# The copies of the bias tables from memory to memory: four parts of two heads instead of one copy of eight

## What is computed

```python
h = rms_norm(x, norm_gain)
proj = h @ w_in              # pool value, pool gate, q, k, v, attention gate: 512 columns each
y_pool = multiscale_pool(pool_v, pool_w, pool_scale) * silu(pool_g)
# each chunk of 64 rows reads itself and 8 chunks before it, 8 heads of 64
s = q @ k.T / 8 + bias[h, clip(j - i, -64, 64) + 64]
y_attn = softmax(masked s) @ v * silu(attn_g)
out = rms_norm(x + concat(y_pool, y_attn) @ w_out, final_norm_gain)
```

## Time and profile before

| | |
|---|---|
| median of 3 runs | 1805.46 us (1803.0 to 1809.53) |
| profiled execution, its own time | 1807.35 us |
| span of the profile | 1805.6 us |
| granted TensorE clock, mean | 0.984 of full speed |
| busy share: TensorE, VectorE, ScalarE, GpSimd | 91%, 59%, 47%, 39% |
| traffic of the DMA engines | 257.84 MB, mean 143 GB/s |

### The profile page before, as it was taken

How to read it: one execution, slowest core, us unless ns; L and a number is a source line. 1 busy time by engine, 2 the same in 40 slices (tenths; PEclk the granted TensorE clock), 3 DMA queues, 4 the chain that set the end, 5 groups by cost and what they waited for, 6 DMA issues and landing times. The chain is left out here.

```text
span 1805.6 us, 43913 instructions
## 1 busy us (share of the span) xinstructions
PE 1644.2 (91%) x17920; PEld 1220.5 (68%) x17920; DVE 1068.5 (59%) x2188; ACT 843.5 (47%) x1580; POOL 708.4 (39%) x734
## 2 busy tenths in 40 slices
PE   5999699999999999999879999999999999999977
PEld 2554345568667676777567787778777787778854
DVE  7767477747456556544355565556655565556654
ACT  5554455422112111111145766567565765667565
POOL 3534345311112121001324644465545654456544
PEclk8999899999999999999989999999999999999999
DMA  5655574462542453244743342442334332442332
GB/s 205 209 204 200 196 247 170 170 251 72 186 164 83 163 187 129 83 159 166 218 147 101 99 131 79 136 131 106 102 106 148 112 125 72 136 148 90 107 94 83
DMA packets 111231, 257.84 MB, mean 143 GB/s; under 512 B 11928, under 2 KB 24744, under 8 KB 108984
## 3 DMA queue, kind: packets, MB, share of 16 engines
q1 hardware_dynamic: 109992, 253.73, 42.0%
q0 software_dynamic: 1040, 1.31, 0.4%
HBM read 151.33 MB, written 83.48 MB: 130 GB/s over the span
## 5 line engine op out<-in xcount | busy, mean ns | idle before, releaser
L2029 POOL TENSOR_TENSOR stages<-stages 128x512 f16<-128x512 f32 (+1 forms) x368 | 379.3, 1046 | 445.3 <-ACT stages L1814 445.1
L1489 PE MATMUL bank<-middle,weights 128*128 128x128 f16 x1792 | 315.0, 220 | 14.0 <-DVE middle L1526 13.1
L1492 PE MATMUL bank<-middle,weights 128*128 128x128 f16 x1792 | 314.6, 220 | 0.0
L1491 PE MATMUL bank<-middle,weights 128*128 128x128 f16 x1792 | 314.5, 220 | 0.0
L1808 ACT ACTIVATE stages<-bank,log_ps 128x512 f32<-128x512 f32 (+1 forms) x368 | 222.0, 603 | 163.9 <-POOL stages L2029 93.4
L1899 DVE CUSTOM_DVE_ANT_0 stages<-bank,stages 128x640 bf16<-128x640 f32 (+4 forms) x256 | 200.0, 781 | 158.2 <-PE bank L1647 157.9
L975 PE MATMUL bank<-middle 128*128 128x256 f16 x784 | 215.7, 275 | 7.5 <-DVE stages L1103 7.5
L977 PE MATMUL bank<-middle 128*128 128x256 f16 x784 | 215.7, 275 | 0.0
L978 PE MATMUL bank<-middle 128*128 128x256 f16 x784 | 215.6, 275 | 0.0
L1677 PE MATMUL bank<-middle 128*128 128x128 f16 (+1 forms) x840 | 169.4, 244 | 46.5 <-ACT stages L1808 41.9
L1814 ACT ACTIVATE stages<-stages 128x512 f16<-128x512 f32 (+1 forms) x368 | 203.5, 553 | 11.7
(11 more groups left out here) (147 smaller groups left out, 3544.3 us busy)
## 6 DMA issues: line engine op xcount, KB each, us to landing
entry<-in_x SPq DMA_DIRECT2D x64, 512.0 KB, 3.6
h_ops<-middle SPq DMA_DIRECT2D x16, 1792.0 KB, 6.1
middle<-h_ops SPq DMA_DIRECT2D x112, 256.0 KB, 5.1
middle<-h_ops SPq DMA_DIRECT2D x49, 512.0 KB, 6.9
middle<-middle SPq DMA_DIRECT2D x192, 128.0 KB, 2.3
residual<-entry SPq DMA_DIRECT2D x32, 512.0 KB, 2.8
entry<-residual SPq DMA_DIRECT2D x30, 512.0 KB, 4.1
out<-entry SPq DMA_DIRECT2D x30, 512.0 KB, 2.9
```

Source lines behind the costliest of these rows:

```text
L1489: nc.tensor.matmul(dst, wh, hop3[:, o, 0, kt, :], start=(kt == 0 and s < 2 and pair == 0), stop=False, skip_group_check=True)
L1491: nc.tensor.matmul(dst, wh, hop3[:, o, 1, kt, :], start=False, stop=False, skip_group_check=True)
L1492: mm = nc.tensor.matmul(dst, wl, hop3[:, o, 0, kt, :], start=False, stop=(kt == 3), skip_group_check=True)
L2029: nc.gpsimd.tensor_tensor(p_l[:, h % 2, c + a:c + b], p32[:, s, a:b], p_h[:, h % 2, c + a:c + b], ALU.subtract).then_inc(A["pl_done"], 1)
```

## The change

The two copies of all eight heads at the end of turn 5 become four pairs of copies of two heads each, at the ends of turns 5, 6, 7 and 8, each at the same place, behind `store_v(p, 1)` and ahead of the next turn's `load_x`. Each DMA is built as before, but its outermost dimension has 2 entries (heads) in place of 8. The semaphore `bias_stored` now reaches 128 instead of 32, and both waits for it ask for that.

```diff
+            def store_bias(h):
+
+                if h == 0:
+                    sp.wait_ge(H["ext_stored"], 16)
+                for r, (dst, width) in enumerate(((bq_dram, 640), (bk_dram, 256))):
+                    sp.dma_start(dst[h:h + 2], bass.AP(rel_dram.tensor, (r * HEADS + h) * EXT + P - 1,
+                                               [[EXT, 2], [-1, P], [1, width]])).then_inc(H["bias_stored"], 16)
...
-                if p == BIAS_AT + 2:
-                    sp.wait_ge(H["ext_stored"], 16)
-                    for r, (dst, width) in enumerate(((bq_dram, 640), (bk_dram, 256))):
-                        sp.dma_start(dst, bass.AP(rel_dram.tensor, r * HEADS * EXT + P - 1,
-                                                  [[EXT, HEADS], [-1, P], [1, width]])).then_inc(H["bias_stored"], 16)
+                if 0 <= p - BIAS_AT - 2 < HEADS // 2:
+                    store_bias(2 * (p - BIAS_AT - 2))
...
-            pool.wait_ge(H["bias_stored"], 32)
+            pool.wait_ge(H["bias_stored"], 16 * HEADS)
...
-            sp.wait_ge(H["bias_stored"], 32)
+            sp.wait_ge(H["bias_stored"], 16 * HEADS)
```

## The result

The changed kernel takes 1856.74 us (median of 4 runs, 1855.41 to 1858.74) against 1806.38 for the one before: ratio 1.028, 95% interval 1.0258 to 1.0302. The forecast was 1855.4. The profiled execution has a span of 1857.0 us, 51.4 more than before, at a mean granted clock of 0.968 instead of 0.984.

What follows compares the result with a forecast made beforehand. TensorE bounds the first stage unless held; the copies' late x load holds it. Three added delays put turn 10 at 48.4 us later, plus 1.5 slow clock: 1807.35 + 49.9 = 1857.3, 1855.4 as a median; range 1836 to 1868.

Steps and rivals of the forecast that it cites:

- One head to an engine: Bias copies: each head's share runs on one engine at 25 GB/s, so a two-head part still takes 19.1 us.
- the first rival: Copy division at line 867: parts keep eight engines or more, each delaying 4.8 us, 1796.5 us as a median; chance 0.08.
- The loop of A, B and C: Turns 6 to 9: three lengths chain each late square to the next store; turn 10 begins 49.9 us later.
- A: From the store of h to the next turn's square: 28.35 us with the copies, 9.60 or 8.89 without.
- B: From that square to the start of TensorE's next turn when it has to wait: 6.47 us.
- C: From TensorE's start of a turn to the next store of h: 2.22 us, some 3.4 in turn 9.
- The fold turn's hole at the transposes: Turn 7, line 240: TensorE's second transposes wait for the copy-out behind the square, starting at 229.5 instead of 214.76.
- The other rivals: Bias parts: two engines run faster than 25 GB/s each, 1817 us, chance 0.04; delays cancel, 1803 to 1809, chance 0.02.
- The lower bound: Least time of a bias part: 0.92 MB over all 16 engines at 393 GB/s, 2.3 us, inside the slack of 3.
- the forecast case: Four parts at turns 5 to 8, each delaying the x load 19.1 us: 1855.4 us as a median; chance 0.86.
- the faster rival: Same as the first rival: eight engines gain 8.9 us by turn 10, all 16 gain 17.5 (1788); chance 0.08.
- What queues behind the part: SyncE's queue: x load, gates store, second x load, in turns 6 and 9 two weight loads; only first x load late.

Runs made afterwards that it cites:

- the single narrow part: Against the kernel before: heads 0 and 1 alone copied at the end of turn 5, other six heads in four 12-wide parts, turns 6 to 9; 1811.32 us, ratio 1.0015.

## Why the prediction was right, step by step

- *One head to an engine, so a part costs its 19 us whatever its bytes.* This step carried the case. Shown by the shares 0.13, 0.26 and 0.51 to 0.52 for two, four and eight heads, by the single narrow part (hole 15.46) and by the same bytes in the shape of eight (holes under 3). The rule on the number of engines in the Trainium skill (page "DMA: Bandwidth & Descriptors", section "Why a DMA increments its semaphore by 16 and not by 1") pointed the same way, and all three shares agree with it; the first rival (eight engines whatever the shape) fell.
- *The loop of A, B and C.* Square of turn 7: forecast 227.3, measured 226.75. Transposes: 229.5 and 229.01. Square of turn 8: 266.4 and 265.45. Turn 9: 272.9 and 271.93. Square of turn 9: 304.3 and 303.06. Turn 10: 310.8 and 309.52. The length A was 0.5, 1.0 and 0.3 us shorter than put, and the stretch from turn 7's transposes to the store of h 0.5 longer (8.77 against 8.27). The sum was 49.9; the mark of turn 10 moved by 49.3, of which 0.5 was there before turn 6 (its first transposes begin at 166.55, before at 166.03). That the two numbers lie so close is in part luck: the start of turn 10 was put 1.3 us too late, and its slow matmuls, put at 1.5 us, cost 2.2 (from 309.52 to the mark are 4.78 us, in the kernel before 2.59).
- *The fold turn's hole at the transposes, behind the copy-out.* Right, 13.38 us at line 240.
- *The other rivals.* Two engines did not run faster: 52 GB/s, 26 each.
- *The lower bound was mis-sized.* I took 393 GB/s for a part over 16 engines, 2.3 us. The run showed 4.3: the rate of the stores was no measure for these copies, which moved 256 to 268 GB/s with all engines busy. It touched no number of the forecast case. The best end of the faster rival (1788) was not reached at these places; 1796 was measured. The other end of that rival, eight engines with 8.9 us gained, was tried and gained 6 to 7: its steps had left out what the lower clock costs behind a short hole.
- *What queues behind the part.* In the changed kernel only the x load was late for anybody, as predicted. In my own expectation for the parts behind the second x load I forgot the weight loads, which the prediction had listed.

The copies' cost in the kernel before, put at 17.5 us, is confirmed by taking them out of the stage: 17 to 18.

## What to carry to other kernels

When a transfer is cut in parts, look at which dimension shrinks. If it is the outermost one, and each of its entries has an engine to itself as here with two, four and eight, each part uses fewer engines and takes as long as the whole, and what is due behind it in that queue is late once for each part. Read the DMA share while the transfer runs alone: 0.52 with eight entries points to it before anything is changed, and one narrow part settles it. Count a short hole of TensorE with what the lower clock adds. And before a transfer is made smaller, look for a place in the same queue with nothing due behind it: here a move of unchanged copies was worth more (1790) than any new shape that was tried (1796 at best).

## What the runs showed of the hardware that was not expected

- A copy from memory to memory ran at 50 GB/s on two engines, 106 on four, 205 on eight, and 256 to 268 on sixteen. The first three are in step with the engines; twice the engines after that gave only 1.3 times the rate, with every engine shown as busy. A full share is therefore not a full rate here.
- The same bytes in the same shape made the x load 4 us late from GpSimd's queue and 19 from SyncE's own. The two queues' copies differed in their packets and in the number of engines busy, so how the engines divide their time between queues is not shown.
- The granted clock fell to 0.50 behind holes of TensorE of only 2.99 and 2.37 us, for 1.5 and 1.7 us of cost each.
